# Attention stage of a two-block transformer kernel: output projection spread between the head pairs, PSUM banks reassigned, two pairs' maxima ahead of the scalings

## Chip, cores and metric

One Trainium2 chip, one of its cores. The metric is device microseconds from start to end of one launch; lower is better.

## What is computed

The reference runs ten stages on one sequence of 256 tokens with 1024 channels: a Conformer-like block (feed-forward, convolution, two feed-forwards, attention, feed-forward) and a second block (mixer, feed-forward, grouped attention, feed-forward). Only the attention stage is touched. With 256 tokens there is one block of 256 keys, so the "mixture of blocks" is plain causal attention with a distance penalty, 8 heads of 128 channels:

```python
k, v = jnp.split(rms_norm(x, g_kv) @ w_kv, 2, axis=-1)
q = (h @ attn_w_q[j]).reshape(B, T, N_HEADS, HEAD_DIM)
s_own = jnp.einsum('bhqd,bhpd->bhqp', qq, k_own, preferred_element_type=jnp.float32)
s_own = jnp.where(d_own >= 0, s_own - slopes4 * d_own.astype(jnp.float32), NEG_INF)
p = jax.nn.softmax(jnp.concatenate([s_sel, s_own], axis=-1), axis=-1)
y = moba_attention(q, kv[0], kv[1], kv[2], slopes) @ attn_w_o[j]
x = x + rms_norm(y, mix_norm_post[layer])
```

## The kernel before

Everything is float32. A product with a weight matrix is made of three matmuls in the format fp32r: the weight is split into a high part `wh` (ScalarE, one copy of 128x2048) and the rest `wl` (VectorE, one subtraction of 128x2048), the activation likewise into `xTh` and `xTl`. All weights come as one stream of 260 pieces of 1 MB into a ring of 7 buffers `raw`; `wl` has 7 buffers too and `wh` has 5. A `Ring` on ScalarE and one on VectorE decide where in each engine's program the splits stand: `ring.need(n)` splits up to piece n, `ring.fill(k, done)` splits up to k pieces as long as the next one is less than 5 beyond `done`. A split of piece p waits for its load and, for the `wh` buffer, until TensorE is done with piece p-5; a load waits until TensorE is done with piece p-7.

Each engine has its own program, written out by hand, and they meet only at semaphores. An engine runs its program strictly in order, so what stands behind a waiting instruction waits too.

The attention stage has pieces p0 to p0+15 (p0 is 111): 4 for values, 4 for keys, 4 for queries, 4 for the output matrix. TensorE first makes the values (`v_part`), turns the normalised input (`turn_in("mixpre1", t)`, eight transposes for each half t of the tokens), then makes keys and queries turned (`project_t`, four heads in a call; `heads_q(0)` and `heads_q(1)` are the two calls for the queries). After that come four pairs of heads. For pair i:

- TensorE `scores(i)`: 8 matmul rows into two banks; VectorE `scores(i)`: adds the penalty and the mask while it copies to `sca`, then takes the maximum of each row, for t = 0 and t = 1
- ScalarE `scores(i)`: four exponentials with their sums; VectorE `scale(i)`: reciprocal and scaling
- TensorE `turn(i)`: six transposes into two banks; ScalarE `turn(i)`: two copies to `PTa`
- TensorE `values(i)`: 8 matmul rows into one bank; ScalarE `values(i)`: copy to `xTh`; VectorE `values(i)`: the rest to `xTl`

The eight banks of PSUM are handed on with `clear(b)`, which waits for whoever empties bank b. Before, `scores(i)` has banks 0 and 1 or 2 and 3 in turn, every `turn(i)` has banks 4 and 5, `values(i)` has bank 6 or 7. The output projection is `close`: eight calls of `down(...)`, one for each chunk q (the channels of pair q, piece p0+12+q) and each half t, 12 matmuls of 512 columns each, results added up in banks 2t and 2t+1. All eight wait for the last pair. Behind the seventh stands `turn_in(AFTER["attn"], 0)`, the transposes for the next stage `d`, whose input of half 0 comes from the results of half 0: `post_stat` (sum of squares, ScalarE), root (GpSimdE), scaling and adding to `x` and scaling by the next gain (VectorE).

The calls themselves, TensorE's loop over the pairs:

```python
for i in range(n_pairs + 3):
    if i < n_pairs:
        scores(i)
    if 2 <= i < n_pairs + 2:
        turn(i - 2)
    if i >= 3:
        values(i - 3)
    if i in beside:
        beside[i]()
```

`beside` is `{1: heads_q(1)}`. VectorE's loop has `scale(i - 1)` ahead of `scores(i)`, a split behind it, then `values(i - 3)`.

## Time and profile before

| | |
|---|---|
| median of 3 runs | 1694.7 us (1694.5 to 1695.89) |
| profiled execution, its own time | 1693.43 us |
| its span, first to last instruction | 1692.1 us |
| busy: TensorE, its weight loads, VectorE, ScalarE | 97%, 79%, 58%, 47% of the span |
| mean granted TensorE clock | 0.990 |
| attention stage with its seams | about 703 to 822 us of the span |

Times are microseconds from the start of the span. The ends of matmuls are modelled, so where one follows another without a stop the distance of their starts is what one costs (a matmul of 512 columns is shown 0.39 us long and the next starts 0.23 us later). A wait is what an engine stood idle before an instruction, and the releaser is who set the semaphore that came last.

### The profile page before, as it was taken

To read this page: it belongs to the slowest core of one execution; us is meant where nothing else is said; L and a number is where in the kernel's file an instruction comes from. 1 tells how busy PE (TensorE), PEld (TensorE's weight loads), DVE (VectorE), ACT (ScalarE), POOL (GpSimd) and SP (SyncE) were. 2 spreads that over 40 slices of the span, in tenths; PEclk is the share of its full clock that TensorE was granted. 3 is DMA by queue.
4 is the path that set the end of the run, shared out by engine and by line. 5 is a ranking of instruction groups with operands and counts; after the bars stand their busy time and mean duration, and the time that the engine had idled before them with its cause. 6 is when DMAs were issued, how large, how long until landed. Compare 5 with 4: busy or idle time off the path is not lost.

```text
span 1692.1 us, 18639 instructions
## 1 busy us (share of the span) xinstructions
PE 1636.3 (97%) x7938; PEld 1337.6 (79%) x7938; DVE 974.4 (58%) x1004; ACT 788.9 (47%) x955; POOL 68.4 (4%) x99
## 2 busy tenths in 40 slices
PE   6999998999999999998999999998999999899999
PEld 5877876788888888797888888976788887578887
DVE  4655676454556454745554556878644447855453
ACT  4535444444345444545443445744544345754342
POOL 1000000100001000100100000010000002000000
PEclk9999998999999999999999999999999999999999
DMA  8545442355446555452554545432555445235451
GB/s 332 190 161 196 174 162 100 125 199 199 174 154 244 188 185 189 166 211 101 196 192 179 196 182 187 154 121 48 190 199 199 174 159 193 75 127 197 176 199 49
DMA packets 51391, 289.33 MB, mean 171 GB/s; under 512 B 14151, under 2 KB 14791, under 8 KB 18026
## 3 DMA queue, kind: packets, MB, share of 16 engines
q1 hardware_dynamic: 50732, 286.84, 46.2%
q8 instruction: 63, 1.03, 0.2%
q10 hardware_dynamic: 576, 1.29, 0.2%
q14 instruction: 20, 0.16, 0.0%
HBM read 287.06 MB, written 1.05 MB: 170 GB/s over the span
## 4 chain that ended last, share of the span: by engine, by line
PE 89%; DVE 5%; ACT 3%; SPq 2%; issue 1%; POOL 1%; DMA 1%; DVEq 0%; ACTq 0%
PE ps L530 85%; PE ps L629 2%; SPq L2794 2%; PE ps L539 1%; DVE wl L1928 1%; ACT wh L1259 1%; ACT scg L1841 0%; DMA gains<-in_rows 0%; POOL st L2681 0%; PE ps L1136 0%; DVE tmp L1959 0%; DVE x L1961 0%; DVE scg L2610 0%; ACT tmp L1278 0%; POOL st L2684 0%
## 5 line engine op out<-in xcount | busy, mean ns | idle before, releaser
L1928 DVE TENSOR_TENSOR wl<-raw,wh 128x2048 fp32r<-128x2048 f32 x260 | 588.8, 2287 | 157.9 <-ACT wh L1259 157.9
L530 PE MATMUL ps<-wh,xTh 128*128 128x512 f32 x1408 | 559.6, 397 | 14.7 <-DVE wl L1928 8.7
L530 PE MATMUL ps<-wh,xTl 128*128 128x512 f32 x1408 | 551.9, 392 | 0.0
L530 PE MATMUL ps<-wl,xTh 128*128 128x512 f32 x1408 | 551.5, 392 | 0.0
L1259 ACT ACTIVATE wh<-raw 128x2048 fp32r<-128x2048 f32 x260 | 488.9, 1908 | 3.5 <-PE ps L530 2.2
L530 PEld LDWEIGHTS ps<-wh,xTh 128*128 128x128 f32 x1408 | 266.4, 189 | 80.6 <-issue 12.0
L530 PEld LDWEIGHTS ps<-wh,xTl 128*128 128x128 f32 x1408 | 266.3, 189 | 56.6
L530 PEld LDWEIGHTS ps<-wl,xTh 128*128 128x128 f32 x1408 | 266.5, 189 | 53.3
L2681 POOL TENSOR_SCALAR st<-st 128x1 f32<-128x1 f32 (+2 forms) x46 | 29.5, 642 | 1436.7 <-ACT tmp L1278 847.3
L1322 ACT ACTIVATE sgf<-ps,st 128x256 f32<-128x256 f32 x22 | 10.4, 474 | 104.1 <-PE ps L530 104.1
L1322 ACT ACTIVATE sge<-ps,st 128x256 f32<-128x256 f32 x22 | 10.4, 474 | 98.9 <-PE ps L530 98.9
L530 PE MATMUL ps<-xTh,wh 128*128 128x256 f32 x192 | 54.6, 284 | 0.0
L530 PE MATMUL ps<-xTl,wh 128*128 128x256 f32 x192 | 54.3, 283 | 0.0
L530 PE MATMUL ps<-xTh,wl 128*128 128x256 f32 x192 | 54.3, 283 | 0.0
L1322 ACT ACTIVATE sgd<-ps,st 128x256 f32<-128x256 f32 x22 | 10.4, 473 | 93.1 <-PE ps L530 93.1
L1322 ACT ACTIVATE sgb<-ps,st 128x256 f32<-128x256 f32 x22 | 10.4, 472 | 93.1 <-PE ps L530 93.1
L1322 ACT ACTIVATE sgc<-ps,st 128x256 f32<-128x256 f32 x22 | 10.4, 473 | 93.0 <-PE ps L530 93.0
L2000 DVE SCALAR_TENSOR_TENSOR hbf<-ps,st,sgf 128x256 f32<-128x256 f32 x22 | 10.6, 484 | 73.6 <-ACT sgf L1322 73.6
L2000 DVE SCALAR_TENSOR_TENSOR hbe<-ps,st,sge 128x256 f32<-128x256 f32 x22 | 10.6, 484 | 73.4 <-ACT sge L1322 73.4
L1322 ACT ACTIVATE sga<-ps,st 128x256 f32<-128x256 f32 x22 | 10.4, 474 | 89.4 <-PE ps L530 89.4
L2000 DVE SCALAR_TENSOR_TENSOR hbd<-ps,st,sgd 128x256 f32<-128x256 f32 x22 | 10.7, 484 | 67.0 <-ACT sgd L1322 67.0
L2000 DVE SCALAR_TENSOR_TENSOR hbc<-ps,st,sgc 128x256 f32<-128x256 f32 x22 | 10.6, 484 | 66.8 <-ACT sgc L1322 66.8
(333 smaller groups left out, 2254.1 us busy)
## 6 DMA issues: line engine op xcount, KB each, us to landing
raw<-in_w SPq DMA_DIRECT2D x260, 1024.0 KB, 4.8
gains<-in_rows SPq DMA_DIRECT2D x18, 512.0 KB, 4.1
x<-in_x ACTq DMA_DIRECT2D x2, 512.0 KB, 8.2
nab<-in_rpb SPq DMA_DIRECT2D x32, 32.0 KB, 2.5
out_x<-x SPq DMA_DIRECT2D x2, 512.0 KB, 2.6
qn<-in_rpb SPq DMA_DIRECT2D x16, 32.0 KB, 2.5
xd<-in_rpb SPq DMA_DIRECT2D x16, 32.0 KB, 2.6
df<-in_cst SPq DMA_DIRECT2D x1, 368.0 KB, 23.5
```

The costliest lines, as they stand in the source:

```text
L530: return pe.matmul(o, lhs, rhs, start=start, stop=stop, skip_group_check=False)
L539: m = pe.transpose(bank(b)[:, width * k:width * k + 128], s, ident[:, :])
L629: m = pe.transpose(bank(b)[:, 256 * ft + 128 * t:256 * ft + 128 * t + 128], r.hb[:, j % 2, t, 128 * ft:128 * ft + 128], ident[:, :])
L1259: act.activation(wh[:, p % RING, :], raw[:, p % RAW, :], ACT.Copy).then_inc(*hi(p))
L1322: act.activation(r.sg[:, j % 2, t, :], bank(ffn_bank(j, t))[:, 0:256], ACT.Silu, scale=stat(("r", name, t))).then_inc(*silu(f, j, t))
L1928: TT(wl[:, p % RAW, :], raw[:, p % RAW, :], wh[:, p % RING, :].bitcast(F32), ALU.subtract).then_inc(*lo(p))
L2000: STT(r.hb[:, j % 2, t, :], bank(ffn_bank(j, t))[:, 256:512], stat(("r", name, t)), r.sg[:, j % 2, t, :], ALU.mult, ALU.mult).then_inc(*pr ...
L2681: pool.tensor_scalar(v, ss, mul, add, ALU.mult, ALU.add).then_inc(*mean(*name))
L2794: sp.dma_start(dst[64 * (r % 2):64 * (r % 2) + 64, r // 2, :, 64 * j:64 * j + 64], src).then_inc(*nab_in[i](i, by=16) if (r, j) == (3, 3) ...
```

## The change

The general functions `attention` and `close` are gone, and the stage's calls are written out on each engine.

- TensorE: `turn(0)` stands in the middle of `heads_q(1)`, `values(0)` and `turn(1)` right behind it, then `scores(2)` and `scores(3)`. The chunks of the output projection, now `out(q, t)`, stand between the pairs and wait for their own pair q alone: (0,0), (1,0), (0,1), (2,0), (3,0), (1,1), (2,1), then the transposes for stage `d`, then (3,1).
- Banks: `scores(i)` has 2i and 2i+1, `turn(0)` has 4 and 5 and the later ones 2 and 3, `values(i)` has 0, 4, 5, 6. The output's banks are 0 to 3 as before.
- VectorE: `scores` of two pairs one behind the other, then their `scale`; for the second two pairs `values(1)` stands between the scalings.
- ScalarE: the exponentials of two pairs one behind the other; the splits of p0+13 and p0+14 stand between the two copies of `heads_q(1)`, p0+15 ahead of `turn(2)`, p0+16 behind the last pair, p0+17 between `post_stat` and `norm_stat`.
- Entry: ScalarE splits p0+5 ahead of `v_part(0, 1)`, as soon as p0 is done with, where it split p0+5 and p0+6 behind it.

No arithmetic instruction is added or taken away. The core of the diff:

```diff
+
+        def moba_turn(i):
+            return 2 if i else 4
+
+        def moba_out(i):
+            return (0, 4, 5, 6)[i]
...
-                for i in range(n_pairs + 3):
-                    if i < n_pairs:
-                        scores(i)
-                    if 2 <= i < n_pairs + 2:
-                        turn(i - 2)
-                    if i >= 3:
-                        values(i - 3)
-                    if i in beside:
-                        beside[i]()
-
-            def close(stage, tag, pairs, first_act):
-                p = FIRST[stage] + PIECES[stage] - 4
-                for t in range(2):
-                    for q in range(4):
-                        if q == 3 and t == 1:
-                            turn_in(AFTER[stage], 0)
-                        on.wait_ge(act_lo, tag, *((pairs - 1,) if isinstance(pairs, int) else (t, 1)))
-                        down(stage, p + q, t, lambda k: (xTh[:, 2 * q + k, t, :], xTl[:, 2 * q + k, t, :]),
-                             q == 0 and first_act is None, q == 3, post_step(stage, t))
-
...
+                def scores(i):
+                    s = 2 * i
+                    clear(s, s + 1)
...
+                def turn(i):
+                    on.wait_ge(made, "moba", i)
+                    for kk in range(2):
+                        b = moba_turn(i) + kk
+                        clear(b)
...
+                        m.then_inc(*turned("moba", i, kk))
+                        emptied[b] = [(copied, "moba", i, kk)]
+
+                def values(i):
+                    b = moba_out(i)
+                    clear(b)
...
+                    m.then_inc(*valued("moba", i))
+                    emptied[b] = [(act_lo, "omoba", i)]
+
+                def out(q, t):
+                    on.wait_ge(act_lo, "omoba", q)
+                    down("attn", p0 + 12 + q, t, lambda k: (xTh[:, 2 * q + k, t, :], xTl[:, 2 * q + k, t, :]), q == 0, q == 3, post_step("attn", t))
...
                 heads_q(0, 4)
-                attention("moba", "attn", 4, 128, [128, 256], q_of, k_of, v_of, {1: lambda: heads_q(1, 6)})
-                close("attn", "omoba", 4, None)
+                scores(0)
+                scores(1)
+                heads_q(1, 6, lambda: turn(0))
+                values(0)
+                turn(1)
+                scores(2)
+                scores(3)
+                out(0, 0)
+                values(1)
+                turn(2)
+                out(1, 0)
+                turn(3)
+                values(2)
+                out(0, 1)
+                values(3)
+                out(2, 0)
+                out(3, 0)
+                out(1, 1)
+                out(2, 1)
+                turn_in(AFTER["attn"], 0)
+                out(3, 1)
...
                 v_part(1, 0)
                 ring.fill(2, p0)
+                ring.fill(1, p0 + 1)
                 v_part(0, 1)
-                ring.fill(2, p0 + 2)
+                ring.fill(1, p0 + 2)
                 turn_in("mixpre1", 0, at.qh)
                 v_part(1, 1)
...
-                heads_q(0, 4)
-                attention("moba", "attn", 4, 128, [128, 256], xTh, used(p0 + 6), lambda i: p0 + (10 if i < 2 else 12), {1: lambda: heads_q(1, 6)})
-                close("attn")
+                ring.need(p0 + 10)
+                heads_q(0, 4, 0)
+                heads_q(0, 4, 1)
+                ring.need(p0 + 12)
+                scores(0)
+                scores(1)
+                ring.fill(1, p0 + 8)
+                turn(0)
+                heads_q(1, 6, 0)
+                ring.fill(1, p0 + 9)
+                ring.fill(1, p0 + 10)
+                heads_q(1, 6, 1)
+                values(0)
+                turn(1)
+                scores(2)
+                scores(3)
+                values(1)
+                ring.need(p0 + 16)
+                turn(2)
+                turn(3)
+                values(2)
+                values(3)
+                ring.fill(1, p0 + 11)
+                ring.fill(1, p0 + 12)
+                post_stat("attn", 0)
+                ring.fill(1, p0 + 13)
+                norm_stat(AFTER["attn"], "attn", 0)
+                turn_in(AFTER["attn"], 0, free=(multiplied, p0 + 14))
+                ring.fill(1, p0 + 14)
+                seam("attn", 1, p0 + 16)
...
-                for i in range(n_pairs + 3):
-                    if 1 <= i <= n_pairs:
-                        scale(i - 1)
-                    if i < n_pairs:
-                        scores(i)
-                    if (tag, i) in ahead:
...
-                attention("moba", "attn", 4, 128, [128, 256], (xTh, xTl), False, alibi, lambda i: p0 + (10 if i < 2 else 12),
-                          {1: lambda: ring.need(p0 + 12)})
-                close("attn")
+                ring.need(p0 + 12)
+                scores(0)
+                scores(1)
+                scale(0)
+                scale(1)
+                ring.fill(1, p0 + 8)
+                ring.fill(1, p0 + 9)
+                ring.fill(1, p0 + 10)
+                values(0)
+                scores(2)
+                scores(3)
+                scale(2)
+                values(1)
+                scale(3)
+                ring.need(p0 + 16)
+                values(2)
+                values(3)
+                ring.fill(1, p0 + 11)
+                ring.fill(1, p0 + 12)
+                seam("attn", 0, p0 + 12)
+                ring.fill(1, p0 + 13)
+                turn_in(AFTER["attn"], 0)
+                ring.fill(1, p0 + 14)
+                seam("attn", 1, p0 + 16)
```

ScalarE, from the copies of `heads_q(0)` (`qT`) on, before; `wh` rows are splits, `sca` rows exponentials:

```order
L1530 ACTIVATE qT<-ps 128x512 x2
L1259 ACTIVATE wh<-raw 128x2048
L1476 ACT_TABLE_LOAD
L1476 ACTIVATE sca,sma<-sca,sma 128x128 x2
L1476 ACTIVATE sca,sma<-sca,sma 128x256 x2
L1259 ACTIVATE wh<-raw 128x2048
L1476 ACTIVATE sca,sma<-sca,sma 128x128 x2
L1476 ACTIVATE sca,sma<-sca,sma 128x256 x2
L1530 ACTIVATE qT<-ps 128x512 x2
L1259 ACTIVATE wh<-raw 128x2048
L1476 ACTIVATE sca,sma<-sca,sma 128x128 x2
L1476 ACTIVATE sca,sma<-sca,sma 128x256 x2
```

and after:

```order
L1470 ACTIVATE qT<-ps 128x512 x2
L1481 ACT_TABLE_LOAD
L1481 ACTIVATE sca,sma<-sca,sma 128x128 x2
L1481 ACTIVATE sca,sma<-sca,sma 128x256 x2
L1481 ACTIVATE sca,sma<-sca,sma 128x128 x2
L1481 ACTIVATE sca,sma<-sca,sma 128x256 x2
L1489 ACTIVATE PTa<-ps 128x512
L1489 ACTIVATE PTa<-ps 128x2x128
L1470 ACTIVATE qT<-ps 128x512
L1256 ACTIVATE wh<-raw 128x2048 x2
L1470 ACTIVATE qT<-ps 128x512
L1494 ACTIVATE xTh<-ps 128x512
```

The two splits between the exponentials are gone, two now stand between the copies of `heads_q(1)`, and the copies of `turn(0)` stand ahead of them.

VectorE, from the first pair's scores on (`L2241` and `L2184` penalty and maximum, `L2166` and `L2169` reciprocal and scaling, `wl` a split), before:

```order
L2241 SCALAR_TENSOR_TENSOR sca<-dm,ps 128x128 x2
L2184 TENSOR_REDUCE sma<-sca 128x2
L2241 SCALAR_TENSOR_TENSOR sca<-dm,ps 128x256 x2
L2184 TENSOR_REDUCE sma<-sca 128x2
L1928 TENSOR_TENSOR wl<-raw,wh 128x2048
L2166 RECIPROCAL sma<-sma 128x2
L2169 TENSOR_SCALAR sca<-sca,sma 128x128 x2
L2166 RECIPROCAL sma<-sma 128x2
L2169 TENSOR_SCALAR sca<-sca,sma 128x256 x2
L2241 SCALAR_TENSOR_TENSOR sca<-dm,ps 128x128 x2
L2184 TENSOR_REDUCE sma<-sca 128x2
L2241 SCALAR_TENSOR_TENSOR sca<-dm,ps 128x256 x2
```

and after (`L2159` and `L2162` penalty and maximum, `L2169` and `L2172` reciprocal and scaling):

```order
L2159 SCALAR_TENSOR_TENSOR sca<-dm,ps 128x128 x2
L2162 TENSOR_REDUCE sma<-sca 128x2
L2159 SCALAR_TENSOR_TENSOR sca<-dm,ps 128x256 x2
L2162 TENSOR_REDUCE sma<-sca 128x2
L2159 SCALAR_TENSOR_TENSOR sca<-dm,ps 128x128 x2
L2162 TENSOR_REDUCE sma<-sca 128x2
L2159 SCALAR_TENSOR_TENSOR sca<-dm,ps 128x256 x2
L2162 TENSOR_REDUCE sma<-sca 128x2
L2169 RECIPROCAL sma<-sma 128x2
L2172 TENSOR_SCALAR sca<-sca,sma 128x128 x2
L2169 RECIPROCAL sma<-sma 128x2
L2172 TENSOR_SCALAR sca<-sca,sma 128x256 x2
```

The second pair's maxima moved ahead of the first pair's scaling, and the split between them moved behind both scalings.

TensorE, from the last pair's scores on (`kT,qT` scores, `ident,sca` turns, `PTa,vv` values, before):

```order
L530 MATMUL ps<-kT,qT 128x128 x2
L530 MATMUL ps<-kT,qT 128x256 x2
L784 MATMUL ps<-ident,sca 128x128 x6
L530 MATMUL ps<-PTa,vv 128x256
L530 MATMUL ps<-PTa,vv 128x128
L530 MATMUL ps<-PTa,vv 128x256
L530 MATMUL ps<-PTa,vv 128x128
L784 MATMUL ps<-ident,sca 128x128 x6
L530 MATMUL ps<-PTa,vv 128x256
L530 MATMUL ps<-PTa,vv 128x128
L530 MATMUL ps<-PTa,vv 128x256
L530 MATMUL ps<-PTa,vv 128x128
```

and after, the last matmuls of `out(0, 0)` (`wl,xTh`, `wh,xTl`, `wh,xTh`), `values(1)`, `turn(2)`, and the first of `out(1, 0)`:

```order
L535 MATMUL ps<-wl,xTh 128x512
L535 MATMUL ps<-wh,xTl 128x512
L535 MATMUL ps<-PTa,vv 128x256
L535 MATMUL ps<-PTa,vv 128x128
L535 MATMUL ps<-PTa,vv 128x256
L535 MATMUL ps<-PTa,vv 128x128
L798 MATMUL ps<-ident,sca 128x128 x6
L535 MATMUL ps<-wh,xTh 128x512
L535 MATMUL ps<-wl,xTh 128x512
L535 MATMUL ps<-wh,xTl 128x512
```

Where turns and values of neighbouring pairs followed each other, twelve matmuls of the output projection now stand on either side.

## Rows read from the trace of the kernel before

**Rows 1.** The page, parts 1 and 6: busy time of each engine; weight loads.
```profile
PE 1636.3 (97%) x7938; PEld 1337.6 (79%) x7938; DVE 974.4 (58%) x1004; ACT 788.9 (47%) x955; POOL 68.4 (4%) x99
...
raw<-in_w SPq DMA_DIRECT2D x260, 1024.0 KB, 4.8
```

**Rows 2.** Waits of TensorE, 700 to 850 us: total us, times, longest.
```profile
PE ps L784 <- ACT PTa L1486: 5.7, 2, 3.6
PE ps L530 <- DVE xTl L2193: 1.4, 1, 1.4
PE ps L539 <- DVE ql L1967: 1.4, 1, 1.4
```

**Rows 3.** Timeline at the stage's entry: start us, us, instruction (xcount).
```profile
722.75 3.71 ACT L1259 ACTIVATE wh<-raw 128x2048 fp32r<-128x2048 f32 x2
...
724.69 4.50 DVE L1928 TENSOR_TENSOR wl<-raw,wh 128x2048 fp32r<-128x2048 f32 x2 [6.02 <-ACT wh L1259]
729.10 1.28 DVE L1967 TENSOR_TENSOR ql<-ps,qh 128x512 fp32r<-128x512 f32 x2
...
729.93 1.16 PE L539 MATMUL ps<-ident,xn 128*128 128x128 f32 x8 [1.38 <-DVE ql L1967]
```

**Rows 4.** Timeline of TensorE, projection of queries to the next stage.
```profile
765.32 2.78 PE L530 MATMUL ps<-kT,qT 128*128 128x128 f32 x16
767.75 0.47 PE L530 MATMUL ps<-qh,wh 128*128 128x256 f32 x1
...
779.30 1.47 PE L530 MATMUL ps<-kT,qT 128*128 128x128 f32 x8
...
784.89 0.85 PE L784 MATMUL ps<-ident,sca 128*128 128x128 f32 x6 [2.15 <-ACT PTa L1486]
785.57 1.47 PE L530 MATMUL ps<-PTa,vv 128*128 128x256 f32 x8
...
791.31 2.65 PE L530 MATMUL ps<-PTa,vv 128*128 128x256 f32 x8
793.76 1.35 PE L784 MATMUL ps<-ident,sca 128*128 128x128 f32 x6
794.95 2.78 PE L530 MATMUL ps<-PTa,vv 128*128 128x256 f32 x16
799.14 0.50 PE L530 MATMUL ps<-wh,xTh 128*128 128x512 f32 x1 [1.41 <-DVE xTl L2193]
...
818.32 1.03 PE L539 MATMUL ps<-ident,xn 128*128 128x128 f32 x8
```

**Rows 5.** Windows: length, busy us (count) by engine, then TensorE's granted clock.
```profile
792.00:794.00 2.00, 2.00 (x9) 1.77 (x8) 1.21 (x6) 0.16 (x1) 0.00 (x0) 0.50 0.00 0
```

**Rows 6.** Timeline of VectorE and ScalarE in the attention and behind it.
```profile
766.83 0.48 DVE L2241 SCALAR_TENSOR_TENSOR sca<-dm,ps 128x128 f32<-128x128 f32 x2 [5.74 <-PE ps L530]
...
771.26 0.16 DVE L2166 RECIPROCAL sma<-sma 128x2 f32<-128x2 f32 x1
...
772.58 0.48 DVE L2241 SCALAR_TENSOR_TENSOR sca<-dm,ps 128x128 f32<-128x128 f32 x2
...
774.81 2.28 DVE L1928 TENSOR_TENSOR wl<-raw,wh 128x2048 fp32r<-128x2048 f32 x1
...
798.40 0.69 DVE L2193 TENSOR_TENSOR xTl<-ps,xTh 128x512 fp32r<-128x512 f32 x1 [0.62 <-ACT xTh L1493]
...
815.11 1.23 DVE L1944 TENSOR_TENSOR xn<-x,gains 128x1024 f32<-128x1024 f32 x1
...
769.23 0.40 ACT L1476 ACTIVATE sca<-sca,sma 128x128 f32<-128x128 f32 x1
...
771.00 1.90 ACT L1259 ACTIVATE wh<-raw 128x2048 fp32r<-128x2048 f32 x1
...
784.17 0.84 ACT L1486 ACTIVATE PTa<-ps 128x512 f32<-128x512 f32 x2
...
810.35 1.03 ACT L1278 ACTIVATE tmp<-ps 128x1024 f32<-128x1024 f32 x1 [11.99 <-PE ps L530]
```

More of the change, by code:

```diff
@@ L434, in build @@
         nab_in = [steps(f"nab{i}") for i in range(4)]
-        ahead = {}
         def split_of(p):
@@ new lines, in values @@
+                def values(i):
+                    b = moba_out(i)
+                    clear(b)
+                    on.wait_ge(copied, "vv", 1, 1)
+                    for kk in range(2):
+                        on.wait_ge(copied, "moba", i, kk)
+                    for hh in range(2):
+                        h = 2 * i + hh
+                        for kk in range(2):
+                            m = mm(bank(b)[:, 256 * hh + 128 * kk:256 * hh + 256], at.vv[:, kk, 128 * h:128 * h + 128],
+                                   r.PT[:, i % 2, kk, hh, 128 * kk:256], kk == 0, kk == 1)
+                    m.then_inc(*valued("moba", i))
+                    emptied[b] = [(act_lo, "omoba", i)]
@@ L1510, in close @@
[L1510 to L1517 removed]
             def attn():
                 p0 = FIRST["attn"]
+                r = rooms["attn"]
                 def v_part(j, t):
@@ L2155, in conv, with attn, scores @@
                 seam("conv", 1, p0 + 12)
-            def attention(tag, stage, n_pairs, M, W, oT, pool, bias, done, beside):
-                r = rooms[stage]
+            def attn():
+                p0 = FIRST["attn"]
+                r = rooms["attn"]
+                def scores(i):
+                    on.wait_ge(scored, "moba", i)
+                    on.wait_ge(const_in["dm"])
+                    if i >= 3:
+                        on.wait_ge(turned, "moba", i - 3, 1)
+                    for t in range(2):
+                        n, a = 128 * (t + 1), 12 * (i % 3) + 6 * t
+                        P = r.sc[:, i % 3, t, :, 0:n]
+                        S = bank(2 * i, 2).rearrange("p (h t n) -> p h t n", h=2, t=2)[:, :, t, 0:n]
+                        for hh in range(2):
+                            v = STT(P[:, hh, :], at.dm[:, t, 0:n], -float(2.0 ** -(2 * i + hh + 1)), S[:, hh, :], ALU.mult, ALU.add)
+                        v.then_inc(*weighed("moba", i, t))
+                        on.wait_ge(weighed, "moba", i, t)
+                        dve.tensor_reduce(r.sm[:, a:a + 2], P, AX.X, ALU.max, negate=True).then_inc(*peaked("moba", i, t))
@@ L2195, in attention @@
-                for i in range(n_pairs + 3):
-                    if 1 <= i <= n_pairs:
-                        scale(i - 1)
-                    if i < n_pairs:
-                        scores(i)
-                    if (tag, i) in ahead:
-                        assert ring.next == ahead[tag, i]
-                        if pool:
-                            ring.next += 1
-                        else:
-                            ring.fill(1, done(i))
-                    if i >= 3:
-                        values(i - 3)
-                    if i in beside:
-                        beside[i]()
@@ L2211, in close @@
[L2211 to L2221 removed]
+                    v.then_inc(*made("moba", i))
+                def values(i):
+                    on.wait_ge(act_hi, "omoba", i)
+                    d = slice(2 * i, 2 * i + 2)
+                    TT(xTl[:, d, :, :], bank(moba_out(i)).rearrange("p (h t n) -> p h t n", h=2, t=2), xTh[:, d, :, :].bitcast(F32), ALU.subtract).then_inc(*act_lo("omoba", i))
```

195 lines of the change are left out of this document (49 added, 146 removed).

## The prediction

> **What bounds the kernel now.** The page first: TensorE is busy for 97% of the span and every other engine for less than 60% [rows 1]. So the time is TensorE's work plus the stretches in which it stands or runs at the lower clock, and only those of the attention stage can change. Its waits there are three kinds [rows 2]: 1.4 us at the entry for `ql`, twice (5.7 us together) ahead of a pair's transposes for ScalarE's copies to `PTa`, and 1.4 us ahead of the output projection for the last `xTl`.
>
> The timeline then gives prices, start to start [rows 4]: scores 2.43 us for two pairs, so 1.22 each; `heads_q(1)` 779.30 - 767.75 = 11.55; a pair's transposes 785.57 - 784.89 = 0.68; a pair's values about 1.3 (16 rows shown as 2.78 with a modelled end); a chunk of the output projection (818.32 - 799.14) / 7 = 2.74; the transposes for the next stage about 0.8. The next stage then starts at 818.32 + 0.8 + 2.74 = 821.9.
>
> From the first scores to there it is 821.9 - 765.3 = 56.6 us. The work at full speed is 4 x 1.22 + 11.55 + 4 x 0.68 + 4 x 1.3 + 8 x 2.74 + 0.8 = 47.1 us. So 9.5 us are lost. Of these, 7.1 are the waits as the trace counts them. 1.65 are a slow stretch: `values(1)` takes 793.76 - 791.31 = 2.45 instead of 1.3 and the next transposes 1.19 instead of 0.68 [rows 4], while the granted clock is 0.50, the level of 1.2 GHz [rows 5]; it followed the longest wait, of 3.6 us [rows 2]. The wait of 2.15 us before it did not have that effect: `values(0)` behind it takes 1.47 as shown, `values(1)` 2.65. The last 0.75 are modelled ends, which make waits look shorter.
>
> **The change, part by part.** Times are on the clock of before.
>
> *Entry.* ScalarE makes the splits of p0+5 and p0+6 from 722.75 on, VectorE the low parts until 729.1, and only then `ql`; TensorE's transposes start at 729.93 [rows 3]. After the change the first split waits for p0 alone, whose last use is 12 matmuls or 2.74 us ahead of the end of `v_part(0, 1)` at about 722.1. So it runs 719.5 to 721.4 and its low part to 723.7. The second runs 722.75 to 724.6 and to 726.9, and `ql` takes 1.28 more [rows 3], to 728.2. TensorE ends its own work at about 728.5. VectorE is 2.2 us earlier and 1.4 are needed, so the wait of 1.4 goes. Nothing is late next: until the pairs TensorE shows no further wait [rows 2], and VectorE stood 5.74 us idle before the first scores [rows 6].
>
> *First two pairs.* VectorE begins the scores at 766.83. One pair's scores cost 774.81 - 772.58 = 2.23 and one scaling 772.58 - 771.26 = 1.32 [rows 6]. With both maxima first, pair 0 is scaled at 766.8 + 4.5 + 1.3 = 772.6. `turn(0)` stands half a projection behind 767.75, at 773.5: covered by 0.9 us, and each us beyond that would cost one. ScalarE's exponentials of a pair (1.77, from 769.23 to 771.00 [rows 6]) run in step with the maxima. Its copies to `PTa` (0.84 [rows 6]) end near 775.1; `values(0)` wants them at 780.0. Two splits of 1.9 us then end at 779.2, a microsecond before the second copy of the queries is due. This is where the 5.7 us of waiting go, and with them the slow stretch.
>
> *Between the pairs.* TensorE does `values(0)`, `turn(1)`, two pairs' scores, until 784.4. The first chunk needs ScalarE's copy and VectorE's remainder of pair 0 (0.6 + 0.69 [rows 6] + 0.25 behind 781.3), ready at 782.9: covered by 1.5. The chunk and `values(1)` last to 788.4. `turn(2)` needs the scaling of pair 2. Its scores reach VectorE at 783.4, and pair 3's maxima now stand ahead of the scaling: 783.4 + 2 x 2.23 + 1.32 = 789.2. So TensorE waits 0.9 us. Queued behind it is `out(1, 0)`, which needs ScalarE's copy of pair 1. That stands behind pair 3's exponentials, which end at 789.0: copied at 789.6, remainder at 790.3, while the transposes end at 790.0. Another 0.35. ScalarE's split of p0+15 ahead of the copies of `turn(2)` delays them to 792.3, under a chunk that lasts to 793.1. The remainders of pairs 2 and 3 come at 796.6 and 800.7 and are wanted at 799.1 and 801.9. The hand-over that cost 1.4 before is covered.
>
> *End.* The transposes for the next stage need the whole chain from the last matmul of half 0. Before, that matmul ended at 799.14 + 4 x 2.74 = 810.1, ScalarE started at 810.35, and VectorE's last step ended at 815.11 + 1.23 = 816.3 [rows 6]: a chain of 6.2 us under three chunks (8.2). After, only two chunks (5.5) stand there, so TensorE waits about 0.75.
>
> *Switches.* No row is added, but float32 rows and fp32r rows alternate more often. The first matmul of the output projection behind such a switch is shown 0.50 long [rows 4] where its like are 0.39; the fp32r side is entered six times instead of two. Bounds are 0 and, were each as dear as a whole matmul of 0.23, 4 x 0.23 = 0.9; I take the row's 4 x 0.1 = 0.4.
>
> *Sum.* 47.1 + 0.9 + 0.35 + 0.75 + 0.4 = 49.5 instead of 56.6 is 7.1 less; with the entry's 1.4, 8.5 us less. The profiled execution took 1693.43, so 1684.9; it was 1.3 below the median of the runs, so the median becomes 1694.7 - 8.5 = 1686.2. Behind the stage all is as before: loads wait for TensorE and move with it.
>
> *A rule against it.* The row says that the clock fell behind 3.6 us of standing and not behind 2.15 [rows 4, 5]; new waits are below 1 us, so by the row no fall is left. The Trainium skill, page "TensorE: Matmul & The Clock Gate", section "A second HAM failure mode: psum-queue depth-cycling", tells of a kernel that cycles through its PSUM banks, whose short stops between groups of matmuls are enough to throw the clock back and forth. By that rule the section, now cut into more small groups with banks handed on, could fall again; this is the second rival.
>
> **Rivals.**
>
> 1. *The forecast*: the waits go, about 2 us come back. 1686.2, with 1683.5 to 1688 as its own range. Chance 0.74.
>
> 2. *The clock falls all the same.* One fall costs 1.65 (above). For it: the section has short rows and three stops. Against it: the fall of before needed the longest stop. One fall gives 1687.9, two 1689.5. Chance 0.14.
>
> 3. *The change does not do what it says*: waits are only moved, from four pairs' copies to the hand-overs between copy, remainder and chunk. One such hand-over is 0.25 + 0.6 + 0.69 and was not hidden before [rows 2, 6]. If all four lay open they would cost 4 x 1.6 = 6.4, leaving 2.1: 1692.6. Against it: covers of 1.5, 2.5 and 1.2 us for three of them. Chance 0.08.
>
> 4. *Slower*: ScalarE stands at the split of p0+13 or p0+14, which is now between the two copies of the queries, because a load is late. Behind it wait the second copy, the copy of pair 0 and all exponentials of pairs 2 and 3, and TensorE for all of them. A load takes 4.8 us [rows 1], and ScalarE split p0+14 at 771.0 without a wait for it [rows 6], while the place is now 777. So the load would have to come more than 1.0 + 8.5 us later than 777 to decide; at 12 us it gives 1697.2. Chance 0.04.
>
> **How the numbers follow.** Predicted is the first case, 1686.2. The best bound is no new waits and no switch cost, 9.5 + 1.4 = 10.9 less, 1683.8, and 0.4 for the spread of the runs: 1683.4. Upwards the range takes in two falls of the clock and half a microsecond: 1690.0. Left out is most of cases 3 and 4 and little of the rest. About 0.2% (3.4 us) is what a measurement of this kernel can tell from no change. Cases 1 and 2 are faster by more, 0.88; case 3 is within it, 0.08; case 4 slower, 0.04.
>
> **What would show it.** Right: no wait for `ql` at the entry; `turn(0)` in the middle of the projection without a wait; a wait of 0.5 to 1.3 ahead of `turn(2)`, one below 0.7 ahead of the chunk behind it, one of 0.5 to 1 ahead of the next stage's transposes with the VectorE row of `xn` as releaser; granted clock 1.00 throughout; first scores to the next stage 49 to 50 us. Wrong: a window at 0.50; a wait ahead of `out(0, 0)`; an idle ScalarE ahead of a split; the next stage's first projections waiting for `xTl`, whose low-part split now starts right behind `xn` and leaves only some 0.1 us. The prediction fails if VectorE is more than 0.9 us late at `turn(0)`, or if the pairs' short rows on TensorE run slower between chunks than they did together.

## The result and the profile after

The changed kernel takes 1684.6 us (median of four runs, 1683.7 to 1686.3) against 1695.0 of the kernel before (four runs, 1694.5 to 1695.9): a ratio of 0.9939 with a 95% interval of 0.9927 to 0.9952. Run again in the experiments it took 1685.6, ratio 0.9942 (0.9928 to 0.9955). The two ratios stand for 10.3 and 9.8 us less; 8.5 were forecast, a ratio of 0.9950, which lies inside both intervals. The profiled execution went from 1693.43 to 1684.72 us, 8.7 less, with a span of 1683.4.

The page of the changed kernel, part 1: busy time of each engine.

```profile
PE 1635.4 (97%) x7938; PEld 1336.7 (79%) x7938; DVE 974.5 (58%) x1004; ACT 789.6 (47%) x955; POOL 70.6 (4%) x99
```

TensorE still does the same 7938 matmuls, and its busy time fell by 0.9 us only [rows 1]. So the gain is not less work: it is time in which TensorE stood, or ran at the lower clock. Its waits from 700 to 850 us say which time that is (us in total, times, longest).

```profile
PE ps L544 <- DVE xn L1934: 1.3, 1, 1.3
PE ps L544 <- DVE xn L1932: 0.6, 1, 0.6
PE ps L798 <- DVE sca L2172: 0.6, 1, 0.6
```

All three rows of [rows 2], four waits, are gone. The first line here is the seam ahead of the stage, as before. The other two are new and were forecast: the scaling of pair 2, and `xn` for the next stage. The timeline of TensorE, from the seam to the next stage (start, length, instruction, and in brackets the idle time before it with what ended it):

```profile
713.08 1.09 PE L544 MATMUL ps<-ident,xn 128*128 128x128 f32 x8 [1.28 <-DVE xn L1934]
...
728.54 1.03 PE L544 MATMUL ps<-ident,xn 128*128 128x128 f32 x8
...
763.81 2.78 PE L535 MATMUL ps<-kT,qT 128*128 128x128 f32 x16
...
772.11 0.82 PE L798 MATMUL ps<-ident,sca 128*128 128x128 f32 x6
...
782.85 0.58 PE L535 MATMUL ps<-wh,xTh 128*128 128x512 f32 x1
...
785.80 1.47 PE L535 MATMUL ps<-PTa,vv 128*128 128x256 f32 x8
787.84 0.87 PE L798 MATMUL ps<-ident,sca 128*128 128x128 f32 x6 [0.57 <-DVE sca L2172]
788.85 0.50 PE L535 MATMUL ps<-wh,xTh 128*128 128x512 f32 x1
...
793.59 0.47 PE L535 MATMUL ps<-wh,xTh 128*128 128x512 f32 x1
...
797.67 0.48 PE L535 MATMUL ps<-wh,xTh 128*128 128x512 f32 x1
...
809.48 1.09 PE L544 MATMUL ps<-ident,xn 128*128 128x128 f32 x8 [0.64 <-DVE xn L1932]
...
813.16 0.39 PE L535 MATMUL ps<-wh,xTh 128*128 128x512 f32 x1
...
821.33 1.03 PE L544 MATMUL ps<-ident,xn 128*128 128x128 f32 x8
...
833.25 0.60 PE L634 MATMUL ps<-ident,hbd 128*128 128x128 f32 x4
```

The window over the pairs and the output projection (length, busy us and count by engine, granted clock, DMA share, GB/s):

```profile
763.80:813.20 49.40, 48.05 (x291) 42.48 (x290) 32.78 (x63) 30.36 (x60) 3.59 (x4) 1.00 0.39 150
```

The granted clock is 1.00 throughout, the level of 2.4 GHz; the stretch at 0.50 of [rows 5] is gone. VectorE, ScalarE and GpSimd in the same stage:

```profile
773.98 3.73 ACT L1256 ACTIVATE wh<-raw 128x2048 fp32r<-128x2048 f32 x2
...
721.69 2.29 DVE L1916 TENSOR_TENSOR wl<-raw,wh 128x2048 fp32r<-128x2048 f32 x1 [2.88 <-ACT wh L1256]
...
727.05 1.28 DVE L1955 TENSOR_TENSOR ql<-ps,qh 128x512 fp32r<-128x512 f32 x2
...
771.09 0.16 DVE L2169 RECIPROCAL sma<-sma 128x2 f32<-128x2 f32 x1
...
780.59 0.69 DVE L2178 TENSOR_TENSOR xTl<-ps,xTh 128x512 fp32r<-128x512 f32 x1 [0.16 <-ACT xTh L1494]
...
813.10 2.29 DVE L1916 TENSOR_TENSOR wl<-raw,wh 128x2048 fp32r<-128x2048 f32 x1 [0.27 <-ACT wh L1256]
816.17 1.28 DVE L1947 SCALAR_TENSOR_TENSOR tmp<-ps,st,gains 128x1024 f32<-128x1024 f32 x1 [0.78 <-POOL st L2656]
...
819.89 2.28 DVE L1916 TENSOR_TENSOR wl<-raw,wh 128x2048 fp32r<-128x2048 f32 x1
...
804.64 0.19 POOL L2653 TENSOR_SCALAR st<-st 128x1 f32<-128x1 f32 x1 [92.94 <-ACT tmp L1275]
...
814.56 0.88 POOL L2653 TENSOR_SCALAR st<-st 128x1 f32<-128x1 f32 x1 [2.25 <-ACT tmp L1275]
```

**Where the time is.** Two instructions that both kernels have stand on either side of the stage: the transposes of the seam ahead of it (713.08 above) and those for half 1 of the next stage (821.33). Call what lies between them the distance: 108.25 us. The kernel before has them at

```profile
712.93 1.09 PE L539 MATMUL ps<-ident,xn 128*128 128x128 f32 x8 [1.28 <-DVE xn L1946]
...
830.12 1.03 PE L539 MATMUL ps<-ident,xn 128*128 128x128 f32 x8
```

a distance of 117.19. The change takes 8.94 us out of it. From there to the end of the span both kernels need the same, 861.98 and 862.07. So the whole gain between these two profiles lies in this stage, and the distance is the sharper measure in the experiments: in the repeated run of the changed kernel it is 108.26.

### The profile page after: what moved, and what is told of

It reads as the page before. It is cut to its first block, busy times and chain, and to the rows that moved or that the text cites. A ratio compares the mean times of both kernels' runs of the same rounds, so it can differ in the third digit from the quotient of the medians.

```text
span 1683.4 us, 18638 instructions
## 1 busy us (share of the span) xinstructions
PE 1635.4 (97%) x7938; PEld 1336.7 (79%) x7938; DVE 974.5 (58%) x1004; ACT 789.6 (47%) x955; POOL 70.6 (4%) x99
## 4 chain that ended last, share of the span: by engine, by line
PE 90%; DVE 6%; ACT 3%; issue 1%; POOL 1%; DMA 0%; SPq 0%; DVEq 0%; ACTq 0%
PE ps L535 86%; PE ps L634 2%; PE ps L544 2%; DVE wl L1916 1%; ACT wh L1256 1%; ACT scg L1829 0%; DVE tmp L1947 0%; DVE x L1949 0%; DMA gains<-in_rows 0%; POOL st L2653 0%; POOL st L2656 0%; PE ps L1133 0%; DVE scg L2582 0%; ACT tmp L1275 0%; DVE smg L2569 0%
## 5 line engine op out<-in xcount | busy, mean ns | idle before, releaser
L2653 POOL TENSOR_SCALAR st<-st 128x1 f32<-128x1 f32 (+2 forms) x46 | 31.7, 688 | 1425.8 <-ACT tmp L1275 837.0
L1319 ACT ACTIVATE sgb<-ps,st 128x256 f32<-128x256 f32 x22 | 10.4, 474 | 93.2 <-PE ps L535 93.2
L1319 ACT ACTIVATE sgd<-ps,st 128x256 f32<-128x256 f32 x22 | 10.4, 475 | 93.1 <-PE ps L535 93.1
L1319 ACT ACTIVATE sgc<-ps,st 128x256 f32<-128x256 f32 x22 | 10.4, 474 | 92.9 <-PE ps L535 92.9
```

The source lines that it names most:

```text
L1319: act.activation(r.sg[:, j % 2, t, :], bank(ffn_bank(j, t))[:, 0:256], ACT.Silu, scale=stat(("r", name, t))).then_inc(*silu(f, j, t))
L2653: pool.tensor_scalar(v, ss, mul, add, ALU.mult, ALU.add).then_inc(*mean(*name))
```

## The experiments

Each edit is made to the changed kernel unless said otherwise. "Distance" is the one above, from the one profiled execution of each kernel; "+" is longer than 108.25. Where no ratio is given, the kernel ran once.

### The changed kernel again

> The changed kernel itself, for a tighter comparison. The two traces account for 7.3 us between the first scores and the next stage (56.6 to 49.35) and 1.5 to 1.7 at the entry, 8.9 together. My theory, that nothing outside the stage takes part: the ratio comes to 1 - 8.9/1695 = 0.9947. Rival, that something else gained 1.5 us more, as the medians so far say: 0.9939 again.

Five runs, no edit: 1685.58 us (1684.0 to 1686.0), before 1694.72, ratio 0.9942 (0.9928 to 0.9955). The interval takes in the theory's 0.9947 and the rival's 0.9939, so it decides for neither. The distance repeats to 0.01 us. The whole time does not repeat that well.

### The entry alone

The kernel before, with the splits of the entry one by one and nothing else:

```
                 ring.fill(2, p0)
+                ring.fill(1, p0 + 1)
                 v_part(0, 1)
-                ring.fill(2, p0 + 2)
+                ring.fill(1, p0 + 2)
```

> The kernel before with the entry's edit alone (split of p0+5 as soon as p0 is done with, p0+6 behind the copy). Theory: the wait for ql (1.4 us as shown, 1.5 start to start) goes and nothing else moves: 1.5 us faster, 0.9991. Rival: the pairs' waits hang on ScalarE and VectorE by themselves, so they grow by what came in earlier and the gain is 0.

1692.93 us, ratio 0.9987 (0.9978 to 0.9996), distance 115.49, which is 1.70 less than before. TensorE's timeline at the entry:

```profile
729.62 1.04 PE L539 MATMUL ps<-ident,xn 128*128 128x128 f32 x8
```

The wait of 1.38 in [rows 3] is gone. All else in the stage, the waits of 5.7 and 1.4 and the slow stretch, stands as in [rows 2]. The entry is a part of its own.

### The entry undone

The same edit taken back in the changed kernel.

> The changed kernel without the entry's edit. Theory: the wait of 1.4 us ahead of the second four transposes of mixpre1 is back, first scores at about 765.4 instead of 763.8, the section behind them 49.35 as in the changed kernel. Rival: the section takes it up and the next stage begins at the same time.

```profile
729.99 1.16 PE L544 MATMUL ps<-ident,xn 128*128 128x128 f32 x8 [1.35 <-DVE ql L1954]
```

The wait returns and the distance is +1.69: the entry is worth 1.7 from either side, and does not depend on the rest. The one run took 1689.0, which is 4.3 more than the profile of the changed kernel and not 1.7. The other 2.7 lie behind the second mark, 864.77 instead of 862.07, in code that this edit does not touch; the last section says what goes with it. That is why the verdicts below go by the distance.

### The chunks behind all pairs

`out(0, 0)`, `out(1, 0)` and `out(0, 1)` stand behind `values(3)`, with `out(2, 0)` and `out(3, 0)` ahead of `out(0, 1)`; the other engines as they are.

```
-                out(0, 0)
                 values(1)
                 turn(2)
-                out(1, 0)
                 turn(3)
                 values(2)
-                out(0, 1)
                 values(3)
+                out(0, 0)
+                out(1, 0)
                 out(2, 0)
                 out(3, 0)
+                out(0, 1)
                 out(1, 1)
```

> The changed kernel with all eight chunks of the output projection behind the last pair, in the order of before; banks, VectorE's and ScalarE's orders stay changed. Theory, that the chunks cover the chains of ScalarE and VectorE: waits of about 1.3 us ahead of values(1), 2.3 ahead of turn(2), 2.2 ahead of turn(3), the end's 0.75 gone; 3.6 us slower than the changed kernel, section 53.0, 5.2 slower if the clock falls. Rival, that the maxima ahead and the new banks make the gain and the chunks' place is indifferent: section within 0.5 of 49.35.

1690.91 us, ratio to before 0.9981 (0.9972 to 0.9990), distance +5.64. TensorE's timeline:

```profile
783.28 1.57 PE L535 MATMUL ps<-PTa,vv 128*128 128x256 f32 x8 [0.38 <-DVE sca L2159]
787.54 1.04 PE L798 MATMUL ps<-ident,sca 128*128 128x128 f32 x6 [2.69 <-DVE sca L2172]
790.20 1.51 PE L798 MATMUL ps<-ident,sca 128*128 128x128 f32 x6 [1.62 <-ACT PTa L1489]
791.51 4.47 PE L535 MATMUL ps<-PTa,vv 128*128 128x256 f32 x16
```

and a window between the second and the third stop:

```profile
788.20:790.00 1.80, 0.38 (x2) 0.00 (x0) 1.73 (x8) 1.80 (x3) 0.00 (x0) 0.50 0.00 0
```

Without the chunks between, TensorE stands 4.7 us in three stops. The clock is at 0.50 already behind the second, of 2.69, ahead of the one of 1.62, and stays there to about 795. The slow `turn(3)` takes 791.51 - 790.20 = 1.31 instead of 0.65, and the 16 rows of values 4.22 up to the next chunk at 795.73 (4.47 as shown) instead of 2 x 1.3: 2.3 us together. So the chunks give back 5.6 of the 7.3 us of the section, some 2.3 of it by the clock. The wait for `xn` at the end, 0.85 start to start, is gone here, since three chunks stand over that chain again: that is what the chunks' new places cost.

### The maxima not ahead

VectorE scales pair 0 ahead of pair 1's maxima, and pair 2 ahead of pair 3's:

```
                 scores(0)
-                scores(1)
                 scale(0)
+                scores(1)
                 scale(1)
...
                 scores(2)
-                scores(3)
                 scale(2)
+                scores(3)
                 values(1)
                 scale(3)
```

> The changed kernel with VectorE's scaling of a pair ahead of the next pair's maxima (scores 0, scale 0, scores 1, scale 1; scores 2, scale 2, scores 3, values 1, scale 3). Theory A, that the order is a trade: the wait ahead of turn(2) (0.8 start to start) goes, but pair 3's exponentials end 1.9 us later, ScalarE's copy of pair 1 stands behind them, and out(1, 0) waits about 3 us instead of 0.35; section 1.8 longer, 51.2; nothing changes for the first two pairs, whose covers are large. Theory B, that two pairs' maxima ahead only cost: section 0.8 shorter, 48.5.

Distance +3.55 (1686.5 in its one run). TensorE's timeline:

```profile
786.52 0.82 PE L798 MATMUL ps<-ident,sca 128*128 128x128 f32 x6
790.25 0.50 PE L535 MATMUL ps<-wh,xTh 128*128 128x512 f32 x1 [2.91 <-DVE xTl L2178]
...
791.85 0.63 PE L535 MATMUL ps<-wh,xTl 128*128 128x512 f32 x1
...
794.69 0.82 PE L798 MATMUL ps<-ident,sca 128*128 128x128 f32 x6
```

The wait ahead of `turn(2)` goes, as it should, and a longer one stands ahead of the chunk behind it: 790.25 - 786.52 - 0.65 = 3.1 start to start, as expected. ScalarE's copy of pair 1 stands behind pair 3's exponentials, which now wait for maxima that come after a scaling. The chunk itself then takes 794.69 - 790.25 = 4.44 us instead of 791.71 - 788.85 = 2.86, with rows of 0.63 where they are 0.39: the clock fell behind a single stop of 2.9 us. The order by itself costs 3.1 less the two waits of the changed kernel here (0.7 and 0.3), 2.0 where 1.8 were expected; the 1.6 us of slow clock come on top and were not expected. Two pairs' maxima ahead of scalings are thus worth 2.0 by the order and 1.6 by the clock.

### A turn in its old banks

`turn(1)` in banks 4 and 5 like `turn(0)`:

```
-            return 2 if i else 4
+            return 2 if i > 1 else 4
```

> The changed kernel with turn(1) in banks 4 and 5 as before (turn 2 and 3 stay in 2 and 3). Theory, that banks matter where the next user stands close behind: scores(2) waits for ScalarE's copies of turn(1), 0.9 to 1.0 us, VectorE's scores start that much later and so does all behind: section 50.3. Rival, that VectorE's chain is the bound there and hides it: within 0.2 of 49.35.

Distance +1.16, and the scores of pair 2 wait for the copies out of these banks:

```profile
780.99 2.86 PE L535 MATMUL ps<-kT,qT 128*128 128x128 f32 x16 [0.89 <-ACT PTa L1489]
```

The banks given out anew are needed for the order, and their price is one hand-over to ScalarE.

### The first turn behind the projection

`turn(0)` stands behind the second `heads_q` and not inside it:

```
-                heads_q(1, 6, lambda: turn(0))
+                heads_q(1, 6)
+                turn(0)
```

> The changed kernel with turn(0) behind heads_q(1) instead of in its middle. Theory, that its place counts through ScalarE's queue: the copies of turn(0), of the queries and the two splits all begin 5.8 us later, values(0) waits 1.1 us, scores(3) waits 1.6 for the second copy of the queries, out(0, 0) is not covered any more; section 2.3 to 3 us longer, 51.7 to 52.3. Rival, that only the wait of values(0) counts: 50.4.

Distance +4.72, with 2.3 to 3 expected. TensorE's timeline:

```profile
779.14 1.55 PE L535 MATMUL ps<-PTa,vv 128*128 128x256 f32 x8 [0.83 <-ACT PTa L1490]
...
783.62 1.58 PE L535 MATMUL ps<-kT,qT 128*128 128x128 f32 x8 [0.96 <-ACT qT L1471]
...
786.47 0.50 PE L535 MATMUL ps<-wh,xTh 128*128 128x512 f32 x1 [1.27 <-DVE xTl L2179]
...
792.23 0.87 PE L798 MATMUL ps<-ident,sca 128*128 128x128 f32 x6 [1.43 <-DVE sca L2173]
```

and ScalarE's:

```profile
778.13 0.87 ACT L1490 ACTIVATE PTa<-ps 128x512 f32<-128x512 f32 x2 [7.43 <-PE ps L798]
...
779.36 3.72 ACT L1257 ACTIVATE wh<-raw 128x2048 fp32r<-128x2048 f32 x2
```

The mechanism is the expected one, ScalarE's queue: its two splits, 3.7 us, begin 5.7 us later than in the changed kernel, counted from the first mark, and the second copy of the queries, pair 0's copy and pair 2's exponentials stand behind them. The two waits that the expectation priced came smaller, start to start 1.0 and 1.2 for 1.1 and 1.6. Missed were the next two: 1.6 ahead of `out(0, 0)` (786.47 - 783.62 - 1.22), which it named without a price, and 0.9 more than in the changed kernel ahead of `turn(2)`. ScalarE had stood 7.43 us idle for one instruction. Four stops of 0.8 to 1.4 follow, and the clock stays at 1.00 through all of them (the window from 776 to 798 us).

### The next stage's transposes inside the last chunk

`turn_in` for the next stage stands in the middle of `out(3, 1)`:

```
-                turn_in(AFTER["attn"], 0)
-                out(3, 1)
+                out(3, 1, lambda: turn_in(AFTER["attn"], 0))
```

> The changed kernel with the transposes for the next stage in the middle of the last chunk instead of ahead of it. Theory, that the next link takes the gain: the wait of 0.75 for xn goes, but VectorE's split of p0+17 stands ahead of xTl and the next stage's first projection waits some 0.5 us; section 0.3 shorter, 49.05. Rival, that the end's wait is free to take: 0.75 shorter, 48.6.

Distance -0.13 (1684.5 in its one run). TensorE's timeline:

```profile
809.63 1.03 PE L544 MATMUL ps<-ident,xn 128*128 128x128 f32 x8
...
812.47 0.50 PE L535 MATMUL ps<-wh,xTh 128*128 128x512 f32 x1 [0.43 <-DVE xTl L1954]
...
822.32 0.50 PE L535 MATMUL ps<-wh,xTh 128*128 128x512 f32 x1 [0.51 <-DVE wl L1915]
```

The wait for `xn` goes, and two others take its place: one for the low part `xTl`, and one behind the second mark, for a split of the next stage's weights. From the first mark to the next stage's first transposes of `hbd` (at 833.25 in the changed kernel) this kernel takes 120.69 us, the changed one 833.25 - 713.08 = 120.17: it lost 0.5. The wait for `xTl` is the expectation's theory; the second wait it did not have.

The chain behind it can be read in the rows of VectorE above, which are alike here. The transposes release ScalarE's copies and the split of a weight behind them, VectorE makes its low part (813.10), then the three steps of half 1's seam (from 816.17), then the low part that TensorE wants (819.89 + 2.28 = 822.2). There is little idle time in it. In the middle of the chunk the transposes start 96.98 us behind the first mark, where they waited for `xn` it was 96.40; the chain, and `hbd` with it, is later by about as much.

### The same, with ScalarE's and VectorE's split first

As above, and the split ahead of half 0's seam on VectorE (shown) and ahead of its `post_stat` on ScalarE:

```
-                seam("attn", 0, p0 + 12)
                 ring.fill(1, p0 + 13)
+                seam("attn", 0, p0 + 12)
```

> As mid_only, and the split of p0+17 moved ahead of post_stat on ScalarE and ahead of the seam on VectorE, where both stood idle. Theory: with the split out of the way xTl is ready when the last chunk ends; section 0.7 to 0.8 shorter than in the changed kernel, 48.6, no wait of TensorE between the last pair and the next stage above 0.1. Rival: the chain runs over ScalarE's statistics, which the split delays, and the section grows.

Distance -0.33 (1685.7 in its one run), where 0.7 to 0.8 were expected. The wait for `xTl` is down to 0.2, that for the weight's split is 0.73, and to `hbd` it is 120.71 us, again 0.5 more than in the changed kernel.

### All waits of the changed kernel taken away

The former edit, and `values(1)` in the middle of `out(0, 0)` on TensorE, ahead of pair 3's exponentials on ScalarE and ahead of the scalings on VectorE, `turn(2)` behind `out(1, 0)`, and `turn(3)` in banks 7 and 4 (TensorE's part):

```
-            return 2 if i else 4
+            return ((4, 5), (2, 3), (2, 3), (7, 4))[i]
...
-                out(0, 0)
-                values(1)
-                turn(2)
+                out(0, 0, lambda: values(1))
                 out(1, 0)
+                turn(2)
                 turn(3)
```

> A version meant to beat both: end_mid, and values(1) in the middle of out(0, 0), out(1, 0) ahead of turn(2), turn(3) in banks 7 and 4 so that turn(2) and turn(3) follow each other, ScalarE's copy of pair 1 ahead of pair 3's exponentials, VectorE's remainder of pair 1 ahead of the scalings. Theory, that the three waits of the changed kernel (0.8, 0.35, 0.8 start to start) were all that was left: 1.6 to 1.9 us less, section 47.5 to 47.8, 0.9936 to before. Rival, that VectorE's chain is the bound and the waits move to values(2) and the last chunks: section 49 or more.

1685.04 us, ratio 0.9939 (0.9926 to 0.9953): as fast as the changed kernel, not faster. TensorE's timeline:

```profile
813.09 0.50 PE L535 MATMUL ps<-wh,xTh 128*128 128x512 f32 x1 [0.18 <-DVE xTl L1953]
...
823.17 0.50 PE L535 MATMUL ps<-wh,xTh 128*128 128x512 f32 x1 [0.72 <-DVE wl L1914]
```

The distance is 0.82 shorter, and the next wait takes it back: to `hbd` it is 120.21 us, in the changed kernel 120.17 (before: 129.10). The expected 1.6 to 1.9 did not come, and not by the rival's way either: the three waits did go. So the stage is bound on two sides now, by TensorE and by the chain of VectorE told above with the transposes inside the last chunk.

### A link of that chain made shorter

One link shows idle time: 0.78 us between the end of the low part, 813.10 + 2.29, and the seam at 816.17, ended by GpSimd's inverse root (`L2653`, `L2656`). GpSimd's first step takes 0.19 us at 804.64, but 0.88 at 814.56, where VectorE works on the low part until 815.4. In this experiment, on top of the former one, VectorE works the root of half 1 out itself. In place of the power stands a product, so the values of that half are not the reference's:

```
-                on.wait_ge(rstd, "post", stage, t)
...
+                on.wait_ge(squared, "post", stage, t)
+                TS(v, stat(("post", stage, t)), m / D, m * 1e-6, ALU.mult, ALU.add).then_inc(*made("pv", stage, t))
+                on.wait_ge(made, "pv", stage, t)
...
+                TS(r, v, -0.5, 1.5, ALU.mult, ALU.add).then_inc(*made("pr", stage, t))
+                on.wait_ge(made, "pr", stage, t)
```

> The kernel with all waits of the changed kernel taken away, and the inverse root for half 1's seam of the attention stage worked out on VectorE instead of GpSimd; the power is replaced by a product there, so the values of this half are not the reference's and only the time is meant. In the trace GpSimd's first step (128 x 1) takes 0.19 us where VectorE does nothing or reads one operand, and 0.85 to 2.3 us where VectorE makes a weight's low part, ending 0.05 us behind it every time. Theory A: the chain behind the last matmul of half 1 sets the next wait, and GpSimd's steps in it cost 0.78 us behind VectorE's split; two steps of 128 x 1 on VectorE itself, each 0.15 as its reciprocals and some 0.2 of waits between, cost 0.4 to 0.5. Then the seam begins 0.3 to 0.4 earlier, TensorE's wait of 0.72 for the weight's low part falls to 0.3 to 0.45, and the distance from the first mark to the next stage's hbd transposes falls from 120.2 to 119.8 to 119.9. Theory B: the seam is not what this split waits for but ScalarE's half of it; then the wait stays at 0.7 and the distance at 120.2.

VectorE and then TensorE:

```profile
813.63 2.29 DVE L1914 TENSOR_TENSOR wl<-raw,wh 128x2048 fp32r<-128x2048 f32 x1 [1.00 <-ACT wh L1254]
815.83 0.15 DVE L1945 TENSOR_SCALAR st<-st 128x1 f32<-128x1 f32 x1
816.01 0.15 DVE L1948 TENSOR_SCALAR st<-st 128x1 f32<-128x1 f32 x1
816.20 1.28 DVE L1955 SCALAR_TENSOR_TENSOR tmp<-ps,st,gains 128x1024 f32<-128x1024 f32 x1
```

```profile
822.26 0.50 PE L535 MATMUL ps<-wh,xTh 128*128 128x512 f32 x1 [0.23 <-DVE wl L1914]
```

From the low part's start to the seam it is 2.57 us instead of 3.08, TensorE's wait falls from 0.72 to 0.23, and to `hbd` it is 119.68 instead of 120.21. That is a little more than theory A wanted, and theory B falls: this chain is what the waits had moved to. How much of the 0.5 is the hold-up by the split and how much the hand-over to GpSimd and back, this experiment doesn't tell apart. The whole time of the one run, 1685.4, doesn't show half a microsecond.

### The same in all twelve seams

Again with a product for the power, so the output is not the reference's.

> The same in all twelve seams that have such a root behind a stage (again with a product for the power, so the output is not the reference's). Theory A: where TensorE waits behind a seam for a weight's low part (3.5 us at 330, 0.7 at 823) some 0.3 to 0.4 goes, elsewhere nothing, since other waits or cover stand there: 0.7 to 1.0 us less than without it, 1684.2, which a ratio can't tell from the changed kernel; the distance as in the single one, 119.8 to 119.9. Theory B: no change in any wait, 1685.0.

1680.78 us (1678.7 to 1682.3), ratio to before 0.9915 (0.9898 to 0.9931), some 4 us less than either kernel with GpSimd's root, where 0.7 to 1.0 were expected. The trace names about half. The wait of 3.5 us for a low part at 330 us falls by 0.5 and the one of this stage by 0.5, as theory A has it; and TensorE's waits of 1.27 and 1.24 for `xn`, at two other seams (714 and 1012 us), fall to 0.83 and 0.82, which the expectation had left out. The rest is not placed, and not all of it need be the root: the profiled executions of this kernel and of the changed one, both with a mean clock of 0.990, took 1682.34 and 1684.72, only 2.4 apart, and the four waits make 1.9 of that. So 1.9 us is what GpSimd's part of these chains is shown to cost in the whole kernel; the medians leave room for some 4. A kernel with the right power on VectorE was not run, so it is no version to use as it stands.

## Why the prediction was right

**The entry**, forecast 1.4: 1.5 from the start of one transposes group to the next (713.08 to 728.54, before 712.93 to 729.93), 1.7 by either experiment. The low part of the first split ends at 721.69 + 2.29 = 724.0 (forecast 723.7), `ql` at 728.3 (forecast 728.2), TensorE arrives at 728.5. The cover is 0.2.

**First scores to the next stage**, forecast 49.5: from 763.81 to the row at 813.16 it is 49.4. Term by term, start to start:
- Ahead of `turn(2)`, forecast 0.9: 787.84 - 785.80 - 1.3 = 0.7. The forecast's own figures, 789.2 against 788.4, give 0.8.
- Ahead of `out(1, 0)`, forecast 0.35: 788.85 - 787.84 - 0.68 = 0.33. The view of waits leaves this one out: the modelled end of the transposes covers it.
- Ahead of the next stage's transposes, forecast 0.75: 809.48 - 797.67 - 4 x 2.74 = 0.85.
- Switches, forecast 0.4: the three chunks that stand alone take 2.95, 2.86 and 2.85 where one in a row takes 2.74, together 0.44.
- The work is then 49.35 - 1.92 - 0.44 = 47.0, where 47.1 were counted.

**The covers.** Pair 0's scaling ends at 771.1 and `turn(0)` starts at 772.1, a cover of 1.0 (forecast 0.9). The remainder of pair 0 ends at 780.59 + 0.69 = 781.3 and the first chunk starts at 782.85, 1.6 (forecast 1.5). The 0.1 left to `xTl` at the next stage held, and the experiment with the transposes inside the last chunk shows how small it is: there it became a wait of 0.4.

**The clock**, forecast to stay: it did, but the reading under it was too simple. The forecast went by the length of the stop (a fall behind 3.6 us, none behind 2.15). Within this stage that holds in all fourteen traces: the ten whose stops are 1.43 us or shorter stay at 1.00, and the four with one of 2.69 or more fall. Elsewhere in the same traces it does not hold. With the entry undone the clock is at 0.50 from 1147.5 us on, right behind a stop of 0.70:

```profile
1147.50:1150.80 3.30, 3.30 (x9) 2.59 (x8) 3.27 (x5) 0.00 (x0) 0.00 (x0) 0.50 0.33 53
```

The changed kernel has the same stop of 0.70 (at 1145.41) and stays at 1.00. It falls behind stops of 2.32 and 1.91 at 1447 and 1457 us; with the transposes inside the last chunk the same two stops are 2.32 and 1.90 and only the first is followed by a fall, and with the first turn behind the projection neither is. So the length alone does not decide, and what does is not shown here. That the stage kept its clock is forecast and in part luck, though it came so ten times out of ten.

The rule of the Trainium skill, page "TensorE: Matmul & The Clock Gate", section "A second HAM failure mode: psum-queue depth-cycling", that frequent short stops between groups of matmuls throw the clock back and forth, was rival 2. In this stage no run bears it out for short stops. The fall behind 0.70 us elsewhere goes the rule's way, so it is not refuted.

**Rivals 3 and 4** did not come: no hand-over between copy, remainder and chunk lies open but the 0.33, and ScalarE shows no idle time ahead of its two splits (the row at 773.98 has no bracket), so no load was late.

**The sum.** 8.5 were forecast, 8.94 are in the distance, 8.7 in the profiled executions. The medians say 10.4 and 9.1, more than the 8.9; nothing in the profiled executions places the difference, since behind the stage both kernels take the same within 0.1 there. It lies within the intervals, and I leave it open.

The parts don't add up, because they share covers: entry 1.7, the chunks 5.6, the maxima 3.6, the turn inside the projection 4.7, the banks 1.2. Each is the price of losing that part from the whole.

## What to carry to other kernels

When one engine is busy for 97% of the span, read the rest start to start, place what it does not need yet between what it waits for, and write for every placed group the instant at which each other engine's queue reaches it; here such a sum came out within 0.2 us on each wait of the forecast. A stop can cost more than its length when TensorE's clock falls behind it: in this stage a single stop of 2.9 us cost 1.6 more, while four of 0.8 to 1.4 cost only themselves. Shorter stops were the safer ones here, not safe ones. Where several waits of half a microsecond are left, follow the chain that ends them before taking them away: three of them went here and the next link, a chain over ScalarE, VectorE and GpSimd, took all of it.

## What the runs showed of the hardware

- **Stops and the clock.** In this stage the granted clock fell to 0.50 behind a stop of 3.6 us (before), one of 2.9, and one of 2.69. It stayed at 1.00 behind 2.15 (before) and through 0.83, 0.96, 1.27 and 1.43 in 15 us. Elsewhere it also fell behind 2.32, 1.91 and 0.70, and not in every run that has the same stop. A fall cost 1.65 (before), 1.6 (the maxima not ahead) and, with a stop of 1.62 in the slow stretch, 2.3 (the chunks behind all pairs). The clock did not drop at once: behind the stop of 2.9 three rows still ran at full speed and the fourth, 0.58 us long, was changing over, and behind 3.6 `values(1)` bears most of it.
- **GpSimd waits for VectorE's splits.** In the changed kernel its first step `L2653` (128 x 1, in a few places 128 x 4 or 128 x 8) takes 0.19 to 0.30 us in 28 places, and 0.85 to 2.30 in the other 18. In each of the 18 a split `wl<-raw,wh`, which reads two operands from SBUF, had begun on VectorE 0.04 to 1.48 us earlier, and GpSimd ended 0.05 or 0.06 us behind it; in none of the 28 did a split run. The Trainium skill, page "SBUF — State Buffer", section "SBUF: two separate sides", says that the two engines share a pair of ports under an exclusive lock, which a VectorE instruction with two SBUF inputs holds to its end. For this direction the trace agrees. The other way round it shows no hold-up: a split that begins 0.18 us into GpSimd's second step at 329.80 takes its usual 2.28 (GpSimd's own spans are rough). The last two experiments show that GpSimd's part of the chain, hold-up and hand-over together, lengthens TensorE's waits here.
- **A chunk of fp32r rows that stands alone between groups of float32 rows** takes about 0.1 us more than one in a row (2.86 and 2.85 against 2.74), the first one 0.2 more (2.95). That the change of format is the reason was not tested apart.
- **The same code is not equally fast in every run, and the clock goes with it.** Behind the second mark nothing was edited but in the last experiment, and the fourteen profiled executions took 860.8 to 864.8 us there. Where the clock stood at 0.50 for 3.4 and 4.3 us of that stretch (the maxima not ahead; the first turn behind the projection) it took 860.8 and 860.9, with 10.2 us (before, changed) 862.0 and 862.1, with 13.7 (all waits away) 863.5, with 14.6 (entry undone) 864.8. A change of one or two microseconds can't be read from one whole time of this kernel; the distance between two marks repeated to 0.01 in the one pair of profiles that tests it.
